# Three norms of a two-layer kernel turned on TensorE by a diagonal of inverse roots, token tile by token tile

## The chip, the cores and the metric

The kernel runs on one core of a Trainium2 chip. Its time is the device time of one execution in microseconds (us), the median of several runs. "Before" is the kernel without the change.

## The reference, cut to what matters

The reference is a transformer layer with attention, a gated delta rule and a product-key expert retrieval, followed by a second layer with two token mixers and a gated feed-forward network. It works on 256 tokens of width 1024. Four times it applies a root-mean-square norm ahead of a large projection:

```python
def rms_norm(x, gain):
    xf = x.astype(jnp.float32)
    y = xf * lax.rsqrt(jnp.mean(xf * xf, axis=-1, keepdims=True) + EPS)
    return (y * gain.astype(jnp.float32)).astype(x.dtype)

h2 = modulate(rms_norm(x, norm2_gain), shift2, scale2)     # h * (1 + scale) + shift, then the expert queries h2 @ w_query
```

The four are: norm 1 (ahead of the first input projection), norm 2 (ahead of the expert queries, with a scale and a shift for every feature), norm 3 (ahead of the second layer's input projection, a gain only) and norm 4 (ahead of the second layer's feed-forward network, a gain only). The change touches norms 2, 3 and 4.

## The kernel before, in words

Tokens are held as two tiles of 128 (tt = 0, 1), with the token on the partition and 1024 features along it. A projection needs its activations with the feature on the partition, so the features are cut into eight K-tiles of 128 (k = 0 to 7), each turned to 128 features by 256 tokens.

**Products in parts.** Every large product is made of three. Both operands are split into a high part, rounded to the type fp32r, and a low part, the rest; high times high, high times low and low times high are summed in PSUM (`three`, L284). The activations' parts are `x_hi` and `x_lo`. The weights arrive in a ring of four chunks, loaded by SyncE (SP). A unit is 128 by 512 weights, and there are eight units for a group of 512 output columns. ScalarE makes a unit's high part (`split_hi`, the copy at L272), VectorE its low part (`split_lo`, the subtraction at L277), into four buffers each. Unit g's buffer is free when TensorE has used unit g - 4. TensorE takes the units in order (`product_group`, L291). In group 0 it waits, ahead of K-tile k, for that K-tile's activation parts (`await_k`) and for the unit's low part (`await_unit`). Each engine's order of work is written out by hand; there is no planner.

**Rows stages.** `rows_stage` (L1265) multiplies row tiles: its output has the tokens on the partition. The last four units are done for token tile 0 first and then for token tile 1, so that VectorE can add tile 0's product to the residual `x` (`add_mix` L1340, `add_wo` L2509, and L1804 and L1805 in the expert stage) while TensorE finishes tile 1. The expert stage has its own code for the same order (L1596 to L1607).

**The norm across a seam.** Each stage is a block of its own. All engines meet where a block ends, before any of them starts the next. At the end of the old block ScalarE loads the table of roots (L456), and then squares each tile of `x` as it becomes ready and takes both square roots in one instruction (L450, L452). In the new block `Norm` does this:

1. VectorE takes both inverses (L472) and scales the rows of tile 0 by its inverse (L474). ScalarE splits unit 0 and then scales the rows of tile 1 (L478).
2. TensorE waits for both (`turn`, L481). It then turns all sixteen 128 by 128 pieces with `pe.transpose` (L362), in four batches of four. A batch is two K-tiles of both token tiles, and a semaphore counts the batches.
3. For each batch, ScalarE writes the high parts of its two K-tiles out of PSUM, with the feature's gain as its scale (L491). Then it splits one weight unit, until four are split. VectorE makes the two low parts (L500; with a shift L505 and L509) and its part of the unit.
4. TensorE starts group 0 as soon as K-tile 0 and unit 0 are there. ScalarE and VectorE go on with unit 4 (`split_groups` L312, and the loops after `norm_his` at L2409 and `norm_los` at L2246).

## Time and profile before

| | |
|---|---|
| time, median of 3 runs (lowest to highest) | 1727.39 us (1727.37 to 1729.22) |
| the profiled execution: its own time, its span | 1728.96 us, 1727.2 us |
| granted TensorE clock over the span | 0.965 of full speed |
| busy, share of the span | TensorE products 92%, weight loads 83%, VectorE 73%, ScalarE 51%, GpSimd 3% |
| three-part products, L287, of 5016 records | 978.6 us busy |
| expert products, L1575, of 3072 records | 386.8 us busy |
| TensorE idle ahead of the turning transposes, L362 | 56.7 us, most of it released by ScalarE's L478 |
| TensorE idle ahead of L287 | 36.5 us, most of it released by VectorE's L277 |

The profile is of one execution. PE is TensorE, PEld its weight loads, DVE VectorE, ACT ScalarE, POOL GpSimd and SP SyncE. "L287" is line 287 of the kernel. A group's line gives the number of records, the busy time, the mean length of one, and then how long the engine sat idle just before them and whose instruction released it. A weight load and a product overlap, and so do successive products, so the mean length of one is more than the distance from one to the next. A plain f32 product leaves two records, a transpose one, and a product of fp32r parts one.

### The profile page before, as it was taken

What the parts mean: (1) busy time and instruction counts of PE and PEld (TensorE: products, weight loads), DVE (VectorE), ACT (ScalarE), POOL (GpSimd) and SP (SyncE); (2) the same over time, 40 slices, a digit from 0 to 9 for tenths busy, and PEclk for the clock granted to TensorE, in tenths of its full rate; (3) what the DMA queues carried; (4) which work ended last, traced back from release to release, by engine and by line L of the source; (5) the groups of instructions that cost most, each with busy time, mean ns of one, the idle gap of its engine ahead of it and who ended that gap; (6) DMA issues with size and microseconds to landing.
All of it is one profiled execution on the core that took longest, in us unless ns stands there. A gap on an engine that the chain in (4) does not pass through costs nothing. (4 is left out here: it accounts for less than half of the span.)

```text
span 1727.2 us, 26513 instructions
## 1 busy us (share of the span) xinstructions
PE 1593.8 (92%) x10380; PEld 1441.4 (83%) x10380; DVE 1257.8 (73%) x2512; ACT 877.8 (51%) x1438; POOL 59.2 (3%) x91
## 2 busy tenths in 40 slices
PE   2997588899999999999999999989999889889989
PEld 2887576799999999998888888888888777789977
DVE  6786877688999899976667766656787566654654
ACT  3436145554554554545555555555555756454443
POOL 0211300000000000000000000020000000000000
PEclk8997789999999999999999999999999899999999
DMA  9744346376766555557777777744444223445542
GB/s 338 268 147 135 104 132 212 99 243 227 235 222 213 181 151 171 149 187 236 240 244 242 243 240 241 250 147 151 149 146 141 73 82 114 146 147 192 176 160 108
DMA packets 112825, 314.45 MB, mean 182 GB/s; under 512 B 8432, under 2 KB 9024, under 8 KB 103232
## 3 DMA queue, kind: packets, MB, share of 16 engines
q1 hardware_dynamic: 101056, 277.03, 48.6%
q10 hardware_dynamic: 10976, 33.63, 5.8%
q0 software_dynamic: 672, 2.12, 0.4%
q8 instruction: 82, 1.34, 0.3%
q14 instruction: 39, 0.32, 0.1%
HBM read 293.86 MB, written 18.89 MB: 181 GB/s over the span
## 5 line engine op out<-in xcount | busy, mean ns | idle before, releaser
L287 PE MATMUL ps<-parts,parts 128*128 128x512 f32 (+1 forms) x5016 | 978.6, 356 | 36.5 <-DVE parts L277 31.0
L287 PEld LDWEIGHTS ps<-parts,parts 128*128 128x128 f32 x5016 | 830.3, 192 | 173.0 <-DVE parts L277 23.7
L272 ACT CAST parts<-lead 128x512 fp32r<-128x512 f32 x940 | 580.5, 621 | 652.7 <-PE ps L287 429.3
L277 DVE TENSOR_TENSOR parts<-lead,parts 128x512 fp32r<-128x512 f32 x940 | 650.2, 698 | 336.9 <-ACT parts L272 333.4
L1575 PE MATMUL ps<-parts,parts 128*128 128x256 f32 x3072 | 386.8, 285 | 4.6 <-DVE parts L277 4.6
L1575 PEld LDWEIGHTS ps<-parts,parts 128*128 128x128 f32 x3072 | 374.1, 192 | 5.6 <-DVE parts L277 5.6
L362 PE MATMUL ps<-lead,mem 128*128 128x128 f32 (+1 forms) x290 | 47.6, 332 | 56.7 <-ACT mem L478 39.7
L362 PEld LDWEIGHTS ps<-lead,mem 128*128 128x128 f32 (+1 forms) x290 | 41.9, 166 | 62.3 <-issue 32.7
L1749 DVE TENSOR_SCALAR mem<-lead,mem 128x128 f32<-128x128 f32 x256 | 71.2, 342 | 0.0
L1561 PE MATMUL ps<-mem 128*128 128x128 f32 x512 | 67.8, 275 | 0.7 <-DVE mem L1749 0.7
L1561 PEld LDWEIGHTS ps<-mem 128*128 128x128 f32 x512 | 62.8, 192 | 1.1 <-issue 1.1
L1746 DVE TENSOR_SCALAR mem<-lead,mem 128x128 f32<-128x128 f32 x256 | 55.6, 281 | 0.0
L1779 DVE TENSOR_TENSOR mem<-mem 128x1024 f32<-128x1024 f32 x32 | 39.0, 1219 | 4.0 <-DMA mem<-act_spill 4.0
L1784 DVE TENSOR_TENSOR parts<-mem,parts 128x1024 fp32r<-128x1024 f32 x32 | 39.0, 1219 | 0.0
L1133 PE MATMUL ps<-mem 64*64 64x64 f32 x512 | 21.0, 251 | 18.1 <-POOL mem L1119 14.4
L1636 ACT COPY mem<-ps 128x512 f32<-128x512 f32 x64 | 37.0, 578 | 0.0
L1632 ACT CAST parts<-mem 128x1024 fp32r<-128x1024 f32 x32 | 33.4, 1045 | 6.6 <-DVE mem L1779 6.6
L1133 PEld LDWEIGHTS ps<-mem 64*64 64x64 f32 x512 | 19.9, 164 | 19.4 <-POOL mem L1119 15.7
L430 DVE SCALAR_TENSOR_TENSOR mem<-mem 128x1024 f32<-128x1024 f32 x27 | 34.5, 1298 | 0.0
L1615 ACT ACTIVATE mem<-ps 128x1024 f32<-128x1024 f32 x32 | 32.6, 1020 | 0.0
L1928 PEld LDWEIGHTS ps<-mem 128*128 128x128 f32 x256 | 29.8, 192 | 0.6
L1928 PE MATMUL ps<-mem 128*128 128x128 f32 x256 | 29.9, 275 | 0.0
(333 smaller groups left out, 969.4 us busy)
## 6 DMA issues: line engine op xcount, KB each, us to landing
lead<-in_peer_expert_down SPq DMA_DIRECT2D x64, 1024.0 KB, 5.6
lead<-in_peer_expert_up SPq DMA_DIRECT2D x64, 1024.0 KB, 5.6
lead<-in_w_in SPq DMA_DIRECT2D x50, 1024.0 KB, 5.1
lead<-in_w_ffn_in SPq DMA_DIRECT2D x22, 1024.0 KB, 5.1
act_spill<-mem ACTq DMA_DIRECT2D x32, 512.0 KB, 5.2
mem<-act_spill ACTq DMA_DIRECT2D x32, 512.0 KB, 3.5
mem<-in_w_ada SPq DMA_DIRECT2D x27, 512.0 KB, 5.2
lead<-in_w_ffn_out SPq DMA_DIRECT2D x11, 1024.0 KB, 4.9
```

The lines of the kernel that those rows point to most:

```text
L272: act.copy(w_hi[g % BUFFERS], st.words(n, u * UNIT, UNIT)).then_inc(hi_ready, 1)
L277: dve.tensor_tensor(w_lo[g % BUFFERS], st.words(n, u * UNIT, UNIT), w_hi[g % BUFFERS].bitcast(F32), ALU.subtract).then_inc(lo_ready, 1)
L287: mm = pe.matmul(o, lhs[a], rhs[b], start=start and i == 0, stop=stop and i == 2, skip_group_check=True, **kw)
L362: last = pe.transpose(o, i, ident[0:i.shape[0], 0:i.shape[0]])
L1133: mm = pe.matmul(ps[rows, bank, u % 4 * HP:(u % 4 + 1) * HP], left[rows, :], right[rows, :], start=True, stop=True)
L1561: mm = pe.matmul(ps[:, 4 + b % 4, j * P:(j + 1) * P], one1[b % 2][:, j, :], one2[b % 2][:, j, :], start=True, stop=True)
L1575: mm = pe.matmul(ps[:, c % 2 * 2 + m // 2, m % 2 * S:(m % 2 + 1) * S], parts[a][:, ms], (x_hi, x_lo)[b][:, k, :], start=k == 0 and i == 0 ...
L1746: one = dve.tensor_scalar(one1[b % 2][:, j, :], iota, pick(0, b * GT + j), None, ALU.is_equal)
L1749: one = dve.tensor_scalar(one2[b % 2][:, j, :], iota, pick(1, b * GT + j), pick(2, b * GT + j), ALU.is_equal, ALU.mult)
L1779: dve.tensor_tensor(got[q % 2], got[q % 2], at(O_R + q * 1024, 1024), ALU.mult).then_inc(s_pr, 1)
L1784: dve.tensor_tensor(a_lo[q], got[q % 2], a_hi[q].bitcast(F32), ALU.subtract).then_inc(s_al, 1)
L1928: mm = pe.matmul(psf[:, 2048 + u * P:2048 + (u + 1) * P], k, q, start=True, stop=True)
```

## The change

A class `TokenNorm` takes the place of `Norm` for norms 2, 3 and 4; norm 1 keeps `Norm`.

- **Roots by tile.** ScalarE squares tile 0 of `x` and takes its root at once, splits weight unit 0 of the next stage, and then does the same for tile 1. All of it is in the old block (`roots`).
- **Diagonals in place of scaled rows.** VectorE takes each tile's inverse and multiplies the 128 by 128 identity by it. It also makes unit 0's low part (`diagonals`, in the old block, behind the two residual sums). The two passes over the rows (L474 and L478) are gone.
- **Turning by products.** In place of sixteen transposes there are sixteen plain f32 products of a 128 by 128 piece of `x` with the tile's diagonal; each turns and scales its piece at once (`turn`). The eight of tile 0 are made at the end of the old block. Four of tile 1 (K-tiles 0 to 3) are made at the start of the new block. The other four are made inside group 0, one behind each of the K-tiles 0 to 3 (`turn_next`).
- **Parts by K-tile.** ScalarE's high part and VectorE's low part are made for one K-tile at a time, each released by a semaphore of that K-tile. Units 1 to 3 are split behind K-tiles 1 to 3, all later units behind K-tile 7 (`his`, `los`). With a shift, VectorE subtracts first and adds the shift in a second instruction.
- In PSUM, K-tiles k and k + 4 share a bank, in banks 4 to 7.

```diff
@@ -308,6 +308,8 @@
                         mm = three(pe, ps[:, c % 2 * 4 + m, 0:S], [w[:, ms] for w in parts],
                                    [a[:, k, :] for a in left], k == 0, k == KT - 1)
                 mm.then_inc(unit_used, 1)
+                if norm and c == 0:
+                    norm.turn_next(pe, k)
         def split_groups(eng, split, at_unit, seg, groups, evacuate, beside=None, done=0):
@@ -387,6 +389,7 @@
         gate1 = at(O_MODS + 2 * D, D)
         c_row = at(O_MODS + 3 * D, D)
         h = at(O_S + D, TT, D)
+        diag = at(O_S, TT, P)
         O_P1 = O_S + 3 * D
         N_P1 = 3 * 512 + 512
         p1 = at(O_P1, TT, N_P1)
@@ -512,6 +515,95 @@
             def await_k(self, pe, k):
                 pe.wait_ge(self.s_lo, k + 1)
+            def turn_next(self, pe, k):
+                pass
+        class TokenNorm:
+            def __init__(self, tag, src, seg, scale, shift=None, less=None):
+                self.src, self.seg, self.scale, self.shift, self.less = src, seg, scale, shift, less
+                (self.s_sq, self.s_std, self.s_inv, self.s_diag, self.s_t, self.s_less, self.s_hi, self.s_lo) = (
+                    lasting_sem(f"{tag}_{n}") for n in (
+                        "squares", "std", "inverse", "diagonals", "transposed", "less_shift", "hi", "lo"))
+            def roots(self, act, s_src):
+                load_roots(act)
+                for tt in range(TT):
+                    act.wait_ge(s_src, tt + 1)
+                    act.activation(h[:, tt, :], self.src[:, tt, :], ACT.Square, accum_out=tiny[:, tt:tt + 1])\
+                        .then_inc(self.s_sq, 1)
+                    act.wait_ge(self.s_sq, tt + 1)
+                    act.activation(tiny[:, 2 + tt:3 + tt], tiny[:, tt:tt + 1], ACT.Sqrt, bias=eps, scale=1.0 / D)\
+                        .then_inc(self.s_std, 1)
+                    if tt == 0:
+                        split_hi(act, self.seg[0], self.seg[1], 0, 0)
+            def diagonals(self, dve):
+                for tt in range(TT):
+                    dve.wait_ge(self.s_std, tt + 1)
+                    dve.reciprocal(tiny[:, 4 + tt:5 + tt], tiny[:, 2 + tt:3 + tt]).then_inc(self.s_inv, 1)
+                    dve.wait_ge(self.s_inv, tt + 1)
+                    dve.tensor_scalar(diag[:, tt, :], ident, tiny[:, 4 + tt:5 + tt], None, ALU.mult)\
+                        .then_inc(self.s_diag, 1)
+                    if tt == 0:
+                        split_lo(dve, self.seg[0], self.seg[1], 0, 0)
+            def column(self, k):
+                return 2048 + k % 4 * 512 + k // 4 * S
+            def bank(self, k):
+                return psf[:, self.column(k):self.column(k) + S]
+            def turn(self, pe, tt, ks):
+                pe.wait_ge(self.s_diag, tt + 1)
+                for k in ks:
+                    col = self.column(k) + tt * P
+                    mm = pe.matmul(psf[:, col:col + P], self.src[:, tt, k * P:(k + 1) * P], diag[:, tt, :],
+                                   start=True, stop=True)
+                    if tt:
+                        mm.then_inc(self.s_t, 1)
+            def his(self, act):
+                for k in range(KT):
+                    act.wait_ge(self.s_t, k + 1)
+                    act.activation(x_hi[:, k, :], self.bank(k), ACT.Identity, scale=self.scale[:, k:k + 1],
+                                   bias=0.0 if self.shift is None else self.shift[:, k:k + 1]).then_inc(self.s_hi, 1)
+                    if 0 < k < AHEAD:
+                        split_hi(act, self.seg[0], self.seg[1] + k, k, 0)
+            def los(self, dve):
+                for k in range(KT):
+                    dve.wait_ge(self.s_hi, k + 1)
+                    rest = x_lo if self.shift is None else self.less
+                    dve.scalar_tensor_tensor(out=rest[:, k, :], in0=self.bank(k), scalar=self.scale[:, k:k + 1],
+                                             in1=x_hi[:, k, :].bitcast(F32), op0=ALU.mult, op1=ALU.subtract)\
+                        .then_inc(self.s_lo if self.shift is None else self.s_less, 1)
+                    if 0 < k < AHEAD:
+                        split_lo(dve, self.seg[0], self.seg[1] + k, k, 0)
+                    if self.shift is not None:
+                        dve.wait_ge(self.s_less, k + 1)
+                        dve.tensor_scalar(x_lo[:, k, :], self.less[:, k, :], self.shift[:, k:k + 1], None, ALU.add)\
+                            .then_inc(self.s_lo, 1)
+            def await_k(self, pe, k):
+                pe.wait_ge(self.s_lo, k + 1)
+            def turn_next(self, pe, k):
+                if k + 4 < KT:
+                    self.turn(pe, 1, (k + 4,))
         class Turn:
@@ -1262,7 +1354,7 @@
-        def rows_stage(tag, seg, chunks, upto, left, dve_part, turn=None, act_after=None, first=None, last=None, beside=None):
+        def rows_stage(tag, seg, chunks, upto, left, dve_part, turn=None, norm=None, s_src=None, first=None, last=None, beside=None):
@@ -1302,6 +1394,8 @@
                     mm.then_inc(s_rows, 1)
                     for i in range(units - 4, units):
                         half(i, 1).then_inc(unit_used, 1)
+                    if norm:
+                        norm.turn(pe, 0, range(KT))
                 @block.scalar
                 def _(act):
@@ -1309,8 +1403,8 @@
                         norm_his(act, turn, seg)
                     for i in range(AHEAD if turn else 0, units):
                         split_hi(act, n0 + i // UPC, g0 + i, i % UPC, 0)
-                    if act_after:
-                        act_after(act)
+                    if norm:
+                        norm.roots(act, s_src)
                 @block.vector
                 def _(dve):
@@ -1329,13 +1423,16 @@
                         else:
                             dve.wait_ge(unit_used, used_value(g0 + units - 1))
                         dve_part(dve, step, tt)
+                    if norm:
+                        norm.diagonals(dve)
         def product_rows(tt, j=0):
             return psf[:, j * 2048 + tt * D:j * 2048 + (tt + 1) * D]
         O_TMP = O_C
-        s_xsum, s_xsq = sem("x1_rows"), sem("x1_squares")
+        s_xsum = sem("x1_rows")
+        norm2 = TokenNorm("norm2", x, n_query, norm_scale, norm_shift, at(O_P1, KT, S))
         def add_mix(dve, step, tt):
@@ -1343,17 +1440,11 @@
             step(dve.tensor_tensor(at(O_TMP + tt * D, D), product_rows(tt), gate1, ALU.mult))
             dve.tensor_tensor(x[:, tt, :], x[:, tt, :], at(O_TMP + tt * D, D), ALU.add).then_inc(s_xsum, 1)
-        def sum_roots(act):
-            load_roots(act)
-            norm_roots(act, h, x, s_xsq, s_xsum)
         def mods_beside_rows(dve, i):
             if i in (5, 7, 9, 11):
                 fill_mods(dve, FILL3 + (i - 5) // 2, FILL3 + (i - 3) // 2)
-        rows_stage("w_out", n_wout, 4, n_query[0] + SLOTS, (x_hi, x_lo), add_mix, Turn("mix1", mix), sum_roots,
+        rows_stage("w_out", n_wout, 4, n_query[0] + SLOTS, (x_hi, x_lo), add_mix, Turn("mix1", mix), norm2, s_xsum,
                    last=lambda sp: load_fills(sp, FILL4 - 3, FILL4), beside=mods_beside_rows)
...
@@ -1404,7 +1494,7 @@
             @block.tensor
             def _(pe):
-                norm2.turn(pe)
+                norm2.turn(pe, 1, range(4))
                 for c in range(4):
                     if c >= 2:
                         pe.wait_ge(s_qv, c - 1)
@@ -1463,7 +1553,7 @@
                     if c and u == 7:
                         scale(c - 1)
-                norm_los(dve, norm2, n_query)
+                norm2.los(dve)
                 split_groups(dve, split_lo, 3, n_query, 4, lambda c: dve.tensor_copy(
                     qrows[:, 0, c * 512:(c + 1) * 512], ps[:, c % 2 * 4, :]).then_inc(s_qv, 1), beside, AHEAD)
                 dve.wait_ge(s_kt, 1)
...
@@ -1605,6 +1696,7 @@
                 mm.then_inc(s_rows, 1)
                 for i in range(2 * P - 4, 2 * P):
                     half(i, 1).then_inc(unit_used, 1)
+                norm3.turn(pe, 0, range(KT))
             @block.scalar
             def _(act):
@@ -1665,8 +1757,7 @@
                         weights_hi(q + 1)
                     if i % 8 == 7 and q + 2 < UG:
                         load_acts(q + 2)
-                load_roots(act)
-                norm_roots(act, h, x, s_xsq, s_xsum)
+                norm3.roots(act, s_xsum)
             @block.vector
             def _(dve):
@@ -1803,6 +1894,7 @@
                         dve.wait_ge(unit_used, used_value(g1 + 2 * P - 1))
                     step(dve.tensor_tensor(x[:, tt, :], psf[:, 2048 + tt * D:2048 + (tt + 1) * D], gate2, ALU.mult))
                     dve.tensor_tensor(x[:, tt, :], x[:, tt, :], x_back[:, tt, :], ALU.add).then_inc(s_xsum, 1)
+                norm3.diagonals(dve)
...
```

Norms 3 and 4 are called in the same way in the second layer's input projection and in the feed-forward stage.

## Rows read from the trace of the kernel before

**Rows 1.** One line of the page's part 5: VectorE's low parts

```profile
L277 DVE TENSOR_TENSOR parts<-lead,parts 128x512 fp32r<-128x512 f32 x940 | 650.2, 698 | 336.9 <-ACT parts L272 333.4
```

**Rows 2.** Timeline where stage `w_out` passes into the query stage: start, length, what [idle before]

```profile
268.22 1.23 DVE L1344 TENSOR_TENSOR mem<-mem 128x1024 f32<-128x1024 f32 x1
...
273.00 3.41 PE L362 MATMUL ps<-lead,mem 128*128 128x128 f32 x16 [6.08 <-ACT mem L478]
...
276.59 3.01 PE L287 MATMUL ps<-parts,parts 128*128 128x512 f32 x12 [0.17 <-DVE parts L509]
...
284.15 8.20 PE L287 MATMUL ps<-parts,parts 128*128 128x512 f32 x35 [0.55 <-DVE parts L277]
```

**Rows 3.** Timeline where the expert stage passes into the second input projection

```profile
1127.61 1.23 DVE L1805 TENSOR_TENSOR mem<-mem 128x1024 f32<-128x1024 f32 x1
...
1130.64 0.17 DVE L472 RECIPROCAL lead<-lead 128x2 f32<-128x2 f32 x1 [1.80 <-PEq L1538]
...
1132.39 3.68 PE L362 MATMUL ps<-lead,mem 128*128 128x128 f32 x16 [6.08 <-ACT mem L478]
...
1133.55 0.84 ACT L491 ACTIVATE parts<-ps,lead 128x256 fp32r<-128x256 f32 x2 [1.21 <-PE ps L362]
...
1134.28 0.62 ACT L272 CAST parts<-lead 128x512 fp32r<-128x512 f32 x1
...
1134.42 0.88 DVE L500 SCALAR_TENSOR_TENSOR parts<-ps,lead,parts 128x256 fp32r<-128x256 f32 x2 [2.22 <-ACT parts L491]
...
1135.72 9.44 PE L287 MATMUL ps<-parts,parts 128*128 128x256 f32 x75
```

**Rows 4.** Timeline where stage `w_o` passes into the feed-forward stage

```profile
1520.26 1.22 DVE L2511 TENSOR_TENSOR mem<-mem,ps 128x1024 f32<-128x1024 f32 x1 [1.50 <-PE ps L287]
...
1525.04 3.48 PE L362 MATMUL ps<-lead,mem 128*128 128x128 f32 x16 [4.81 <-ACT mem L478]
...
1528.17 14.03 PE L287 MATMUL ps<-parts,parts 128*128 128x256 f32 x113
```

**Rows 5.** Short windows in the three seams: the field PEclk is the granted clock

```profile
269.20:269.80 0.60, 0.00 (x0) 0.00 (x0) 0.24 (x1) 0.32 (x1) 0.00 (x0) 0.50 1.03 410
...
276.00:276.50 0.50, 0.41 (x4) 0.17 (x2) 0.50 (x3) 0.50 (x3) 0.00 (x0) 0.99 0.28 74
...
1129.30:1129.60 0.30, 0.00 (x0) 0.00 (x0) 0.00 (x0) 0.30 (x1) 0.00 (x0) 0.57 0.00 0
...
1136.00:1136.40 0.40, 0.40 (x5) 0.40 (x4) 0.40 (x2) 0.40 (x3) 0.33 (x2) 0.79 0.00 0
...
1528.40:1528.80 0.40, 0.40 (x4) 0.40 (x4) 0.40 (x2) 0.40 (x2) 0.00 (x0) 0.62 0.00 0
```

**Rows 6.** Groups of products by line and form, then two lines of VectorE scalars

```profile
L1928 PE MATMUL ps<-mem 128*128 128x128 f32 x256 | 29.9, 275 | 0.0
...
L1166 PE MATMUL ps<-mem 128*128 128x128 f32 x16 | 3.8, 431 | 0.8 <-DVE mem L1232 0.8
...
L1746 DVE TENSOR_SCALAR mem<-lead,mem x256: 274/280/293, 576.9 to 754.7; 128x128 f32<-128x128 f32 x128
...
L2111 DVE TENSOR_SCALAR mem<-mem x8: 404/405/407, 1194.0 to 1196.9; 128x256 f32<-128x256 f32 x8
```

**Rows 7.** Timeline where the projection stage ends: TensorE last before the block's end

```profile
1462.63 4.06 PE L287 MATMUL ps<-parts,parts 128*128 128x512 f32 x17
...
1467.01 1.94 PE L362 MATMUL ps<-lead,mem 128*128 128x128 f32 x16 [0.32 <-PEq L1870]
```

**Rows 8.** Two idle spells of TensorE and the windows with the clock after

```profile
327.36 1.09 PE L362 MATMUL ps<-lead,mem 128*128 128x128 f32 x8 [2.00 <-DVE mem L1450]
...
325.00:330.00 5.00, 1.70 (x14) 1.23 (x13) 4.25 (x9) 2.39 (x6) 0.00 (x0) 1.00 0.00 0
...
1384.72 3.08 PE L362 MATMUL ps<-lead,mem 128*64 128x128 f32 x16 [2.69 <-DVE mem L2219]
...
1385.00:1390.00 5.00, 5.00 (x25) 4.18 (x23) 4.97 (x8) 4.60 (x8) 0.00 (x0) 0.66 0.61 210
```

More of the change, by code:

```diff
@@ L1389, in build @@
                 "qT_dve", "qT_act", "scores", "scores_dve", "scores_act", "steps"))
-        norm2 = Norm("norm2", h, x, norm_scale, norm_shift, at(O_P1, KT, S))
         with nc.Block() as block:
@@ L1495, in beside @@
                         roots(c - 1)
-                norm_his(act, norm2, n_query)
+                norm2.his(act)
                 split_groups(act, split_hi, 4, n_query, 4, lambda c: act.copy(
@@ L1527, in build @@
         n1, g1 = n_up
-        (s_xsum, s_xsq, s_ld, s_rd0, s_rd1, s_pr, s_ah, s_al, s_rows, s_udv) = (sem("up_" + n) for n in (
-            "x_rows", "x_squares", "x_loaded", "acts_loaded0", "acts_loaded1", "weights", "weights_hi", "weights_lo",
+        (s_xsum, s_ld, s_rd0, s_rd1, s_pr, s_ah, s_al, s_rows, s_udv) = (sem("up_" + n) for n in (
+            "x_rows", "x_loaded", "acts_loaded0", "acts_loaded1", "weights", "weights_hi", "weights_lo",
             "rows_done", "steps"))
@@ L1814, in build @@
         O_W = O_P2 + TT * N_P2
-        norm3 = Norm("norm1_2", h, x, gain_cols[:, 2, :])
         HH = 8
@@ L2011, in heads @@
                     mm.then_inc(s_h, 1)
-                norm3.turn(pe)
+                norm3.turn(pe, 1, range(4))
                 for c in range(G_V):
@@ L2244, in gated @@
                         one.then_inc(norm_hg.s_h, 1)
-                norm_los(dve, norm3, n_in2a)
+                norm3.los(dve)
                 for v in range(AHEAD, V_H):
@@ L2407, in weights @@
                     act.activation(zT[j % 2], zT[j % 2], ACT.Exp).then_inc(s_w, 1)
-                norm_his(act, norm3, n_in2a)
+                norm3.his(act)
                 for v in range(AHEAD, V_H):
@@ L2505, in build @@
                    first=mix_hg)
-        s_xsum, s_xsq = sem("x3_rows"), sem("x3_squares")
+        s_xsum = sem("x3_rows")
+        norm4 = TokenNorm("norm2_2", x, n_ffi, gain_cols[:, 3, :])
         def add_wo(dve, step, tt):
             dve.tensor_tensor(x[:, tt, :], x[:, tt, :], product_rows(tt), ALU.add).then_inc(s_xsum, 1)
-        rows_stage("w_o", n_wo, 4, n_ffi[0] + SLOTS, (x_hi, x_lo), add_wo, Turn("mixed_rows", mixed), sum_roots)
-        norm4 = Norm("norm2_2", h, x, gain_cols[:, 3, :])
+        rows_stage("w_o", n_wo, 4, n_ffi[0] + SLOTS, (x_hi, x_lo), add_wo, Turn("mixed_rows", mixed), norm4, s_xsum)
         ff = at(O_F, FT, S)
@@ L2529, in _ @@
             def _(pe):
-                norm4.turn(pe)
+                norm4.turn(pe, 1, range(4))
                 for c in range(2 * FT // 4):
@@ L2554, in high @@
                     act.copy(ff_hi.piece(t), ff[:, t:t + n, :]).then_inc(s_fh, 1)
-                norm_his(act, norm4, n_ffi)
+                norm4.his(act)
                 hi_groups(act, n_ffi, 2 * FT // 4, evacuate, AHEAD)
@@ L2580, in low_part @@
                                       ALU.subtract)
-                norm_los(dve, norm4, n_ffi)
+                norm4.los(dve)
                 lo_groups(dve, n_ffi, 2 * FT // 4, evacuate, AHEAD)
```

1 line of the change is left out of this document (added).

## The prediction

> **What bounds the kernel now.** I read the page's groups first: TensorE works 92% of the span, almost all of it three-part products, so time is lost where it stands still. The waits by releaser then name the spells. Most of its idle time ahead of transposes is put down to ScalarE's L478, which occurs only in the norms. Last I read the timeline of the three seams that the change touches. In the seams of norms 2, 3 and 4 TensorE idles 6.08, 6.08 and 4.81 us [rows 2 to 4]. The stretch from the end of the second residual sum to the first product of group 0 is what the norm costs: 269.45 to 276.59, 1128.84 to 1135.72, and 1521.48 to 1528.17, thus 7.14, 6.88 and 6.69 us [rows 2 to 4]. After that TensorE sets the pace; only in norm 2 does it stall again, and K-tile 4 starts at 284.15 there, 7.56 us after K-tile 0. So the change is priced by one question per norm: when does K-tile 4 start?
>
> **Part by part: up to the first product.** Let E be the end of the second residual sum (VectorE: 269.45, 1128.84, 1521.48). ScalarE has tile 0's root by then, since its square can start when the first sum ends, 2.6 us earlier. VectorE takes the inverse, 0.17 us [rows 3], and the diagonal, a 128x128 scalar pass of 0.28 us [rows 6]. With three handovers of 0.04 us (TensorE starts 0.04 after L478 ends) TensorE starts tile 0 at E + 0.56. ScalarE's second square and root, and VectorE's second diagonal, run beside it and cost nothing as long as tile 0 takes over about 1.5 us; without that cover the second diagonal would come at about E + 2.1.
>
> A 128x128 f32 product takes 29.9/128 = 0.234 us at full clock and 3.8/8 = 0.475 us at the low level, 1.2 GHz, two records each [rows 6]. In a transpose there is less: 1.94/16 = 0.12 us at full clock [rows 7]. The eight thus take 1.87 or 3.80 us. Which? TensorE fell idle at 266.92 and 1126.31; the clock had fallen by 269.20 and at about 1129.35, that is 2.3 and 3.0 us later [rows 5]. Nothing in the change moves these two moments, and tile 0 starts at 270.01 and 1129.40, behind both. The clock came back 3.0, 3.8 and 3.7 us after TensorE had restarted, at 276.0, 1136.17 and 1528.7 [rows 2 to 5]. I take seven products low and one full, 7 x 0.475 + 0.234 = 3.56 us, for norms 2 and 3. In norm 4 there is only one residual pass, so the spell shrinks from 4.81 to 1.22 (the pass) + 0.04 + 0.56 = 1.8 us, less than the 2.00 us at which the clock stayed at 1.00 [rows 8]; the eight take 1.87 us there.
>
> The Trainium skill, "TensorE: Matmul & The Clock Gate", section "Terms", says that transpose mode is four times faster for FP32. The rows give a factor of 2 at equal clock, so the measurement decides. By the page's factor, from a transpose of 0.12, a turning product would be 0.48 at full clock, and the sixteen would add some 4 us per norm.
>
> The block then ends with TensorE last. Where it was last before, the next block's first instruction came 0.32 us after its modelled end [rows 7]. That end lies 0.16 behind the last issue (record of 0.275 less the spacing of 0.117, rows 6). So the new block begins at B = E + 0.56 + 3.56 + 0.48: 274.05 and 1133.44, and for norm 4 with 1.87 at 1524.39.
>
> TensorE makes K-tile 0 of tile 1 in 0.12 + 0.275, ScalarE starts 0.04 later and makes the high part in 0.48 (two take 0.84), VectorE the low part in 0.48 (two take 0.88) [rows 3], and with 0.03 and 0.07 of handovers the first product is at B + 1.5. TensorE's four own products need only 0.94 of it. In norm 2 the shift is a further 0.41 [rows 6] and 0.03. First products: 276.0, 1134.9, 1525.9. They were at 276.59, 1135.72 and 1528.17, so 0.6, 0.8 and 2.3 us are won. The old K-tile 0 began at the low level for its first 0.45 and 0.53 us in norms 3 and 4, which cost half of that; this also goes, 0.2 and 0.3 us.
>
> **Inside group 0.** Four products stand behind K-tiles 0 to 3 in TensorE's own order: 4 x 0.234 = 0.94 us. Nothing hides them, as TensorE has no idle time there. ScalarE has 0.37 + 0.62 per K-tile, VectorE 0.48 + 0.70, with the shift 1.6, against TensorE's 1.5 + 0.23; they keep up.
>
> Then comes a wait that the old order did not have. Unit 4 is split only behind `his` and `los`, whose K-tile 7 needs the last turning product, which TensorE issues behind K-tile 3. Behind this waiting instruction in ScalarE's queue stands `split_hi` of unit 4, and TensorE's K-tile 4 waits for that. Before, the cast of the next unit followed each batch, and unit 4 was ready early. The chain from the end of the issue: 0.16 + 0.04 to ScalarE, 0.37 (half of 1134.28 - 1133.55) to its next instruction, cast 0.62 [rows 3], 0.03, VectorE 0.70 [rows 1], 0.07: 1.98 us idle. In norm 2 VectorE is last: 0.2 + 0.48 + 0.03 + 0.48 + 0.03 + 0.41 + 0.70 + 0.07 = 2.4 us. From K-tile 4 on nothing differs, and the earlier stalls of norm 2 are in the 7.56 us.
>
> **The sum.** Norm 2: 276.0 + 4 x 1.41 (six products, 8.20/35 each, rows 2) + 0.94 + 2.4 = 284.95 against 284.15: +0.8. Norm 3: -0.8 - 0.2 + 0.94 + 1.98 = +1.9. Norm 4: -2.3 - 0.3 + 0.94 + 1.98 = +0.3. Together +3.0 us. The removed passes L474 and L478 are inside these differences. No DMA moves but by the same few tenths; the chunks in question had landed before.
>
> The profiled execution took 1728.96 us, 1.76 beyond its span; it would take 1732.0. The median is 1.6 lower, so I forecast 1727.4 + 3.0 = 1730.4 us.
>
> Bounds of what no row shows. Turning products between fp32r products could hide their weight loads better or worse than in a row of their own: four at 0.12 (a transpose) to 0.475 (the low level) give -0.5 to +1.0 per norm. ScalarE and VectorE read the banks that TensorE writes at that time, which no row has: from 0 to one more product length per K-tile, 0 to 0.9 per norm; I take 0, the four reads of rows 3 having run beside transposes. The one wait per K-tile in place of one per two costs 0 to 4 x 0.04.
>
> **The rivals.**
> 1. The clock does not fall ahead of tile 0. For it: with a restart after 3.1 us the fall may come too late, depending on where in the spell the chip judges it, and 2.00 us left it at 1.00. Against: 2.69 us of idle was followed by a low stretch [rows 8], and both moments in rows 5 lie ahead of the restart. Then norms 2 and 3 are each 1.69 us earlier: 3.0 - 3.4 = -0.4, 1727.0 us, no change.
> 2. The slower side: the new stall at K-tile 4 drops the clock. Idle of 2.00 us left it up, 2.69 us did not [rows 8]; my stalls are 2.0, 2.0 and 2.4 us, so it decides from somewhere between. The window behind the 2.69 us had 0.66, which is 3.4 of 5 us at half rate; TensorE has no slack there and loses 1.7 us each time. Two of three give 3.0 + 3.4: 1733.8 us.
> 3. The change gains as it stands: unit 4 is ready without that wait, because something in the order lets it through. Then 6.4 us of stall go from the sum: -3.4, 1724.0 us. Against it stands the order of instructions itself; ScalarE takes its queue in order in every row.
>
> **How the numbers follow.** Forecast case 0.50, from 1729 to 1732.5; no fall ahead of tile 0 0.20; clock dropped by the stall 0.20; no stall 0.07; the rest 0.03, of either sign. A measurement of this kernel can tell about 0.2%, 3.5 us, from no change. The forecast lies just inside that bound: of its 0.50 I put 0.22 beyond it, and the second rival's 0.20 too, so slower 0.42. Faster is the third rival and half of the rest with a little of the first: 0.10. Same is what is left, 0.48. The range takes in the first rival and its bounds and the second with two or three drops: 1725.5 to 1735.
>
> **What would show it.** Eight f32 product pairs on the new turning line ahead of each block's end, at a PEclk of about 0.5 in norms 2 and 3 and 1.0 in norm 4; the first product of group 0 some 6.5, 6.1 and 4.4 us behind the second residual sum; a turning product behind each of K-tiles 0 to 3; and an idle spell of about 2 us on TensorE ahead of K-tile 4, released by VectorE's L277. The prediction is wrong if that spell is missing or under 1 us, if the turning products take 0.4 us at full clock, or if the clock drops behind the spell.

## The result and the profile after

| | before | changed |
|---|---|---|
| time, median of 22 runs each | 1729.18 us | 1737.97 us |
| lowest to highest | 1724.75 to 1733.54 us | 1729.51 to 1743.32 us |
| ratio to before, 95% interval | | 1.0048 [1.0036, 1.006] |
| the profiled execution: own time, span | 1728.96 us, 1727.2 us | 1742.69 us, 1741.0 us |

The change makes the kernel slower by 0.48%, 8.3 us by the ratio. The forecast was 3.0 us slower, 1730.4 us from a median of three runs. With 22 runs the kernel before has a median of 1729.2 us, so 1.8 us of the miss in the absolute time is that base, and the rest is the change itself.

From the page of the changed kernel, its span and two groups: records and their shapes, busy time, mean ns of one, idle time ahead and its releaser. The first group line answers to the table of the kernel before, the second to [rows 1].

```profile
span 1741.0 us, 26617 instructions
...
L287 PE MATMUL ps<-parts,parts 128*128 128x512 f32 (+1 forms) x5016 | 985.6, 358 | 42.2 <-DVE parts L277 36.3
...
L277 DVE TENSOR_TENSOR parts<-lead,parts 128x512 fp32r<-128x512 f32 x940 | 650.5, 699 | 337.6 <-ACT parts L272 334.0
```

TensorE's idle time ahead of the three-part products grew from 36.5 to 42.2 us. VectorE's low parts cost what they did.

The timeline of the seam of norm 2 (start, length, what, and in brackets the idle time before it and who ended it), which answers to [rows 2]:

```profile
268.90 1.22 DVE L1441 TENSOR_TENSOR mem<-mem 128x1024 f32<-128x1024 f32 x1
...
270.58 3.78 PE L570 MATMUL ps<-mem 128*128 128x128 f32 x16 [2.97 <-DVE mem L554]
...
274.66 2.05 PE L570 MATMUL ps<-mem 128*128 128x128 f32 x8 [0.30 <-PEq L1364]
...
275.46 1.02 ACT L579 ACTIVATE parts<-ps,lead 128x256 fp32r<-128x256 f32 x2 [3.83 <-PE ps L570]
...
276.99 1.65 PE L287 MATMUL ps<-parts,parts 128*128 128x512 f32 x6 [0.28 <-DVE parts L596]
...
283.31 0.38 PE L570 MATMUL ps<-mem 128*128 128x128 f32 x2
...
284.19 2.17 ACT L272 CAST parts<-lead 128x512 fp32r<-128x512 f32 x4
...
285.11 2.49 DVE L277 TENSOR_TENSOR parts<-lead,parts 128x512 fp32r<-128x512 f32 x4
...
285.94 14.37 PE L287 MATMUL ps<-parts,parts 128*128 128x512 f32 x55 [2.26 <-DVE parts L277]
288.16 0.62 ACT L272 CAST parts<-lead 128x512 fp32r<-128x512 f32 x1 [1.81 <-PE ps L287]
...
290.56 0.62 ACT L272 CAST parts<-lead 128x512 fp32r<-128x512 f32 x1 [1.78 <-PE ps L287]
...
291.95 0.62 ACT L272 CAST parts<-lead 128x512 fp32r<-128x512 f32 x1 [0.77 <-PE ps L287]
```

E, the end of the second residual sum, is 268.90 + 1.22 = 270.12. Tile 0's products start 0.46 behind it, take 3.78 us (low clock), and the first product of group 0 comes at E + 6.87. Behind the last turning product TensorE stands idle for 2.26 us until VectorE has unit 4's low part. Then the reader is to look at ScalarE's casts at 288.16, 290.56 and 291.95. Each is released by TensorE's use of a unit. Two of them are 2.40 us apart and the next two 1.39, so in the first of these two intervals TensorE ran at about half its rate. The clock fell at about 286.9, 0.9 us after TensorE had restarted.

The seam of norm 3, to be read beside [rows 3]: TensorE's pieces and two casts.

```profile
1134.34 3.78 PE L570 MATMUL ps<-mem 128*128 128x128 f32 x16 [2.97 <-DVE mem L554]
...
1138.42 1.97 PE L570 MATMUL ps<-mem 128*128 128x128 f32 x8 [0.30 <-PEq L1629]
...
1140.27 1.70 PE L287 MATMUL ps<-parts,parts 128*128 128x256 f32 x12
...
1149.06 16.12 PE L287 MATMUL ps<-parts,parts 128*128 128x256 f32 x120 [1.89 <-DVE parts L277]
...
1153.46 0.62 ACT L272 CAST parts<-lead 128x512 fp32r<-128x512 f32 x1 [1.89 <-PE ps L287]
...
1155.14 0.62 ACT L272 CAST parts<-lead 128x512 fp32r<-128x512 f32 x1 [1.05 <-PE ps L287]
```

And that of norm 4, beside [rows 4]:

```profile
1534.74 2.05 PE L570 MATMUL ps<-mem 128*128 128x128 f32 x16 [1.71 <-DVE mem L554]
...
1537.09 1.13 PE L570 MATMUL ps<-mem 128*128 128x128 f32 x8 [0.30 <-PEq L1364]
...
1538.63 1.70 PE L287 MATMUL ps<-parts,parts 128*128 128x256 f32 x12 [0.42 <-DVE parts L589]
...
1547.42 12.82 PE L287 MATMUL ps<-parts,parts 128*128 128x256 f32 x105 [1.89 <-DVE parts L277]
```

In norms 3 and 4 the wait ahead of K-tile 4 is 1.89 us. Short windows behind the three waits show the clock (the field behind the four engines' busy times and counts, as in [rows 5]):

```profile
286.60:290.10 3.50, 3.50 (x11) 2.67 (x10) 1.70 (x3) 0.62 (x1) 0.00 (x0) 0.54 0.31 75
...
1151.00:1154.30 3.30, 3.30 (x19) 3.30 (x18) 0.88 (x2) 1.19 (x2) 0.00 (x0) 0.57 0.72 215
...
1547.40:1551.00 3.60, 3.58 (x30) 3.60 (x31) 2.38 (x4) 1.77 (x4) 0.00 (x0) 1.00 0.20 30
```

It was 0.54 and 0.57 of full speed behind the waits of norms 2 and 3, and 1.00 behind that of norm 4.

From the profiles I took the length of each seam: from E to the start of VectorE's low part of unit 12, where both kernels are in the same steady state again.

```
us                   norm 2  norm 3  norm 4   sum     against before
before               22.52   21.03   20.94   64.49
changed              25.27   24.83   21.38   71.48    +7.0
units_early          21.18   21.34   19.25   61.77    -2.7
before_held          25.42   22.71   23.66   71.79    +7.3
before_held_long     26.00   24.78   25.68   76.46   +12.0
tile0_late           22.38   22.45   22.85   67.68    +3.2
after_filled         23.65   23.45   21.38   68.48    +4.0
before_shift         23.45   20.72   20.86   65.03    +0.5
units_early_warm     19.13   19.18   19.26   57.57    -6.9
before_warm          23.93   21.48   21.46   66.87    +2.4
before_warm_short    22.32   19.90   19.89   62.11    -2.4
held_filled          23.78   22.68   22.92   69.38    +4.9
norm4_alone          22.51   21.24   22.88   66.63    +2.1
```

This is one profiled execution of each, so the table shows mechanisms and the timed runs show sizes. What a low stretch behind the wait is worth can be read from pairs with the same order of work, one with and one without it: 25.27 - 23.65, 24.83 - 23.45 and 22.88 - 21.38, thus 1.4 to 1.6 us. Of the 13.7 us between the profiled executions of before and changed, 7.0 lie in the three seams. Most of the rest lies in later stages that the change doesn't touch: from unit 12 of the queries to the expert stage 59.39 against 57.26, in the rest of the second input projection 231.84 against 230.40, and from there to norm 4's second residual sum 101.61 against 99.10. There too it is the clock: its mean in these three stretches is 0.91 against 0.97, 0.95 against 0.96 and 0.98 against 1.00, because low stretches stand at other idle spells.

Every timed execution has its mean granted clock as well. I call 2 x (1 - clock) x span its low time, the time at the lower level. Averaged over the executions it is 118.7 us for the changed kernel (22 of them). For the kernel before, in the three later sets of runs, it is 115.2, 113.3 and 112.9 us (17, 35 and 26 executions). Within one kernel its standard deviation is 5 to 15 us, so an average of twelve is good to some 2 to 4 us. A TensorE at half its rate loses half of that time where it has work to do.

### The profile page after: what moved, and what is told of

Read it like the earlier page. It is cut to its first block and busy times, and to the rows that moved or that the text cites. A ratio compares the mean times of both kernels' runs of the same rounds, so it can differ in the third digit from the quotient of the medians.

```text
span 1741.0 us, 26617 instructions
## 1 busy us (share of the span) xinstructions
PE 1610.4 (92%) x10428; PEld 1455.7 (84%) x10428; DVE 1257.9 (72%) x2518; ACT 875.5 (50%) x1438; POOL 57.3 (3%) x91
## 5 line engine op out<-in xcount | busy, mean ns | idle before, releaser
L287 PE MATMUL ps<-parts,parts 128*128 128x512 f32 (+1 forms) x5016 | 985.6, 358 | 42.2 <-DVE parts L277 36.3
L277 DVE TENSOR_TENSOR parts<-lead,parts 128x512 fp32r<-128x512 f32 x940 | 650.5, 699 | 337.6 <-ACT parts L272 334.0
L364 PE MATMUL ps<-lead,mem 128*128 128x128 f32 (+2 forms) x242 | 37.6, 319 | 39.4 <-ACT mem L481 22.6
L364 PEld LDWEIGHTS ps<-lead,mem 128*128 128x128 f32 (+2 forms) x242 | 32.9, 157 | 43.7 <-issue 32.8
```

The costliest lines, as they stand in the source:

```text
L277: dve.tensor_tensor(w_lo[g % BUFFERS], st.words(n, u * UNIT, UNIT), w_hi[g % BUFFERS].bitcast(F32), ALU.subtract).then_inc(lo_ready, 1)
L287: mm = pe.matmul(o, lhs[a], rhs[b], start=start and i == 0, stop=stop and i == 2, skip_group_check=True, **kw)
L364: last = pe.transpose(o, i, ident[0:i.shape[0], 0:i.shape[0]])
```

## The experiments

**units_early.** Units 4 to 7 are split where units 1 to 3 are; the loops behind start at unit 8.

```diff
-                    if 0 < k < AHEAD:
-                        split_hi(act, self.seg[0], self.seg[1] + k, k, 0)
+                    if k:
+                        split_hi(act, self.seg[0] + k // UPC, self.seg[1] + k, k % UPC, 0)
...
-                for v in range(AHEAD, V_H):
+                for v in range(KT, V_H):
```

> The changed kernel with one thing different: in norms 2 to 4, weight units 4 to 7 are split behind K-tiles 4 to 7, as units 1 to 3 are behind theirs, and not all behind K-tile 7. Theory 1 (the wait at K-tile 4 and the low clock behind it are the loss): the idle spells of 2.26, 1.89 and 1.89 us ahead of K-tile 4 go, 6.0 us, and with them the low stretches that follow some of them, 1.7 us each. Against the changed kernel's 1738.0 that gives 8 to 9 us less, 1729 to 1730; counted from the kernel before and the seams alone it would be 1729.2 + 3.0 - 6.4 = 1725.8. Rival (the loss is in the turning products, or in low stretches far from the seams that have nothing to do with the wait): at most the 6.0 us of idle time, 1732 or more, and low stretches in group 0 as before.

Measured: 1730.79 us (12 runs), ratio to before 1.0006 [0.9989, 1.0023]. TensorE's timeline at K-tile 4 of norm 2 has no gap left; the last turning product is issued 0.14 us ahead of K-tile 4's first:

```profile
282.90 0.38 PE L570 MATMUL ps<-mem 128*128 128x128 f32 x2
283.04 17.29 PE L287 MATMUL ps<-parts,parts 128*128 128x512 f32 x75
```

Its seams are 9.7 us shorter than the changed kernel's. By the ratios to before it is 0.42% faster, 7.3 us. That lies between the 8 to 9 us of theory 1 and the at most 6.0 of the rival, so the time alone doesn't decide; that no low stretch is left in group 0 speaks for theory 1. The wait at K-tile 4 and what follows it are the loss; taken away, nothing is left that can be told from before. The count from the seams alone, 1725.8, was too good: the seams are 2.7 us shorter than before, and the total is not. In its profile the three later stretches named above took 59.94, 232.03 and 101.72 us, 6.9 us more than before, at the same lower clocks as in the changed kernel.

**before_held and before_held_long.** The kernel before, computing the same, with a wait at the same place in each of norms 2, 3 and 4 and nothing else of the change (256 or 1024 columns in the copy; norm 2's is shown):

```diff
                 norm_his(act, norm2, n_query)
+                act.wait_ge(unit_used, used_value(n_query[1] + 3))
+                act.copy(at(O_S, 256), at(O_CONST, 256))
```

> The kernel before with one wait added in each of norms 2, 3 and 4: ScalarE splits unit 4 only when TensorE has used unit 3, behind a copy of 128x256 that nobody reads (0.4 us). It computes the same. That holds TensorE ahead of K-tile 4 for about 0.2 + 0.4 + 0.62 + 0.03 + 0.70 + 0.07 = 2.0 us, as the changed kernel does, with nothing else of the change. Theory 1 (a wait of this length also brings the low clock in part of the cases): 3 x 2.0, less norm 2's own earlier waits, and up to 3 x 1.7: 1729.2 + 8.5 = 1737.7, with low stretches seen behind one or two of the three waits. Rival (the wait costs its own length only): 1735.2 and PEclk 1.00 behind all three.

> The same with a copy of 128x1024 (1.0 us), so that TensorE is held about 2.6 us ahead of K-tile 4 in each of norms 2 to 4. Theory 1: the low clock follows all three waits, 3 x (2.6 + 1.7) = 12.9: 1742, which is 4 to 5 above the shorter hold although the waits are only 1.9 us longer together. Rival: 1.9 us above the shorter hold.

Measured: 1738.69 us (6 runs), 1.0067 [1.0055, 1.0079], and 1741.32 us (6 runs), 1.0082 [1.0067, 1.0097]. The timeline of before_held at norm 2 has the added copy and a wait of 1.83 us:

```profile
282.44 0.40 ACT L1499 COPY mem<-lead 128x256 f32<-128x256 f32 x1 [4.17 <-PE ps L287]
...
284.23 8.01 PE L287 MATMUL ps<-parts,parts 128*128 128x512 f32 x27 [1.83 <-DVE parts L277]
```

Windows right behind the three waits of before_held (PEclk as before), and then of before_held_long, whose waits are 2.47 us:

```profile
284.90:288.40 3.50, 3.50 (x10) 2.69 (x9) 1.68 (x3) 0.64 (x2) 0.00 (x0) 0.51 0.45 113
1146.30:1149.80 3.50, 3.49 (x29) 3.50 (x30) 2.36 (x4) 1.66 (x4) 0.00 (x0) 1.00 0.17 30
1541.20:1544.70 3.50, 3.49 (x29) 3.50 (x30) 2.36 (x4) 1.66 (x4) 0.00 (x0) 1.00 0.15 30
```

```profile
281.50:285.00 3.50, 3.50 (x9) 2.79 (x10) 1.61 (x3) 1.20 (x3) 0.00 (x0) 0.53 0.23 34
1145.00:1148.50 3.50, 3.50 (x19) 3.50 (x19) 0.92 (x3) 1.24 (x2) 0.00 (x0) 0.52 0.64 205
1544.20:1547.70 3.50, 2.81 (x13) 2.84 (x14) 2.35 (x4) 1.39 (x3) 0.00 (x0) 0.52 0.00 0
```

In these profiles the clock was low behind one of three waits of 1.83 us and behind all three of 2.47. before_held loses 11.6 us where its waits add 1.28 + 1.83 + 1.83 = 4.9 us (in norm 2 there was a stall of 0.55 before). That is more than theory 1's 8.5 and far above the rival's 6.0. Its low time is 127.4 us against 115.2 for before in the same set of runs, 12.2 more, and half of that is 6.1. A wait of this kind costs more than its length, and alone it costs at least as much as the whole change. The longer wait didn't separate theory 1 from its rival: it is 2.6 us above the shorter one, where 4 to 5 were expected and the rival said 1.9, the intervals overlap, and its low time is no longer (125.9 us).

**tile0_late.** As units_early, with tile 0's products moved into the new block.

```diff
-                    if norm:
-                        norm.turn(pe, 0, range(KT))
...
+                norm2.turn(pe, 0, range(KT))
                 norm2.turn(pe, 1, range(4))
```

> As units_early, but token tile 0's eight turning products stand at the start of the new block, ahead of the four of tile 1, and not at the end of the old one. Theory 1 (the early tile gains what the seams were worked out to gain): the new block then begins when the second diagonal is there, 2.35 us behind the second residual sum, and the first product of group 0 comes at 2.35 + 3.6 + 1.5 = 7.4 us in norms 2 and 3 (6.9 in the changed kernel, both at the low clock) and at 5.7 to 7.4 in norm 4 (4.3): 2.4 to 4 us above units_early. Rival (the early tile gains nothing, as the same eight products stand in TensorE's way wherever they are): within 1 us of units_early.

Measured: 1734.9 us (6 runs), 1.0037 [1.0023, 1.0051], 0.31% or 5.4 us above units_early. In norm 2 all twelve products start 4.87 us after TensorE fell idle, and the first product of group 0 is 1.2 us later than in units_early (276.56):

```profile
272.01 4.95 PE L570 MATMUL ps<-mem 128*128 128x128 f32 x24 [4.87 <-PEq L1364]
277.76 1.66 PE L287 MATMUL ps<-parts,parts 128*128 128x512 f32 x6 [0.80 <-DVE parts L596]
```

So the early tile does gain something: the seams say 5.9 us and the totals 5.4, where 2.4 to 4 were expected, though the two intervals just touch. In norm 4 the longer idle spell let the clock fall; that seam alone grew by 3.6 us.

**after_filled.** The changed kernel, with products that nobody reads in the wait:

```diff
                 if k + 4 < KT:
                     self.turn(pe, 1, (k + 4,))
+                if k == 3:
+                    for _ in range(14):
+                        pe.matmul(psf[:, 1792:2048], x_hi[:, 0, 0:P], x_hi[:, 0, :], start=False, stop=True, skip_group_check=True)
```

> The changed kernel with TensorE kept busy in the wait ahead of K-tile 4: behind the last turning product, fourteen 128x256 products of fp32r parts (0.12 us each, 1.7 us) into an unused corner of PSUM that nobody reads. The wait itself stays, 1.9 to 2.3 us until unit 4's low part is there. Theory 1 (part of the loss is the low clock that follows the idle spell): no low stretch behind the three waits, so up to 1.7 us less for each that had one; the seams of norms 2 and 3 (25.3 and 24.8 us from the second residual sum to the low part of unit 12) fall to about 23.5 and 23.1, the total by 2 to 5 us, to 1733 to 1736. Rival (the wait costs its own length and nothing else): 1738 as the changed kernel.

Measured: 1732.78 us (12 runs), 1.0014 [0.9999, 1.0029]. K-tile 4 of norm 3 waits as long as before, but TensorE is idle for 0.22 us of it only:

```profile
1143.57 1.92 PE L609 MATMUL ps<-parts 128*128 128x256 f32 x14
1145.71 19.55 PE L287 MATMUL ps<-parts,parts 128*128 128x256 f32 x161 [0.22 <-DVE parts L277]
```

Against the changed kernel, by the ratios to before, that is 0.34%, 5.9 us less (the two intervals together leave some 3 us on either side), with the same waits in the order of work. What is left above before is 2.4 us, and the sum of the prediction, which has no low stretch behind the new wait, was 3.0. This is the run that splits the loss: about 6 us are the clock behind the wait, about 3 the rest. The granted clocks of the single executions agree. Low time was 118.7 us on average over the 22 executions of the changed kernel and 106.8 us over the 12 of this one, 11.9 us less, and half of that is 6.0 us. The Trainium skill, "TensorE: Matmul & The Clock Gate", section "Terms", puts the penalty at about the throttled time multiplied by one less the clock ratio. Here the two agree, 6.0 by the clocks and 5.9 by the times.

The 3 us that are left are not free of the clock. In the kernel before, the clock was low for 3.4 us in norm 4's transposes, and in the changed kernel it is not (the table's 21.38 us has no low stretch); the prediction's sum counts that as a gain. All in all this run has 6.5 us less low time than before in the same set of runs (106.8 against 113.3). By half of it, an estimate, the order of work alone costs nearer to 6 us, and a better clock gives 3 of them back.

**held_filled.** before_held with the same fill, behind K-tile 3.

```diff
                 mm.then_inc(unit_used, 1)
+                if norm and c == 0 and k == 3 and norm is not norm1:
+                    for _ in range(14):
+                        pe.matmul(psf[:, 1792:2048], x_hi[:, 0, 0:P], x_hi[:, 0, :], start=False, stop=True, skip_group_check=True)
```

> before_held (the kernel before, with K-tile 4 held some 2.0 us in norms 2 to 4) with the fourteen 128x256 products that nobody reads behind K-tile 3 in TensorE's order, so that the wait is of the same length and TensorE is busy in it. Theory 1: what before_held loses beyond the waits themselves is the low clock, so this one loses 5.3 (the growth of idle time ahead of K-tile 4 in the three seams): 1729.5 + 5.3 = 1734.8 or a ratio of 1.003, against 1.0067 for before_held. Rival (the held unit costs more than its wait in some other way, such as units split late behind it): 1.006 to 1.007 as before_held.

Measured: 1734.08 us (9 runs), 1.0031 [1.0016, 1.0047], as theory 1 had it. Norm 2 of it:

```profile
283.35 1.83 PE L313 MATMUL ps<-parts 128*128 128x256 f32 x14
285.34 14.98 PE L287 MATMUL ps<-parts,parts 128*128 128x512 f32 x65 [0.17 <-DVE parts L277]
```

The wait is the same and costs 5.4 us now in place of 11.6. The same fill gives back 6 us in a kernel that has nothing of the change but the wait. That the 5.4 are the waits' own 4.9 is less sure than it looks: low time is 106.6 us, against 127.4 in before_held, but also against 112.9 for before in the same set of runs. So here too some clock was gained that before didn't have, and something else, which no run names, took it back.

**before_shift.** A copy of 1.0 us behind norm 2's roots.

```diff
             norm_roots(act, h, x, s_xsq, s_xsum)
+            if s_xsum is x1_sum:
+                act.copy(at(O_S + D, 1024), at(O_CONST, 1024))
```

> The kernel before with one copy of 128x1024 (1.0 us) more on ScalarE behind norm 2's roots, so that everything from norm 2 on comes 1.0 us later, and nothing else. Theory 1a (what the changed kernel loses outside the three seams comes from low stretches that move when the stages behind are moved): the total changes by 1.0 plus or minus 1.7 or 3.4, and the low stretches of the later stages stand elsewhere than in the kernel before. Rival (the difference outside the seams is chance between executions): 1.0 us more on average, 1728.8 to 1730, with the same spread.

Measured: 1729.62 us (12 runs, 1724.86 to 1736.26), 1.0003 [0.9986, 1.0019]; seam of norm 2 0.93 us longer. Inconclusive: the interval holds no effect and the 1.0 us, and no later stage of its profile differs by more than about 0.4 us from before. That merely moving the later stages costs time is not shown.

**units_early_warm.** units_early, with TensorE kept busy ahead of tile 0's products.

```diff
                     for i in range(units - 4, units):
                         half(i, 1).then_inc(unit_used, 1)
+                    if norm:
+                        for _ in range(12 if seg == n_wout else 7):
+                            pe.matmul(psf[:, 2048:2560], left[0][:, 0, 0:P], atr(O_X_HI, KT * S)[:, 0:512], start=True, stop=True)
```

> units_early with TensorE kept busy in the spell ahead of tile 0's turning products: 128x512 products that nobody reads, twelve in norms 2 and 3 (2.6 us) and seven in norm 4 (1.5 us), behind the stage's last product. Theory 1 (the low clock makes tile 0's eight products 3.8 in place of 1.9 us in norms 2 and 3): first product of group 0 about 1.7 us earlier in both, seams of 19.5, 19.6 and 19.3 us, 1730.8 - 3.5 = 1727.3 and less if later low stretches go too. Rival (the fill stands in TensorE's queue ahead of the turning products and eats what the clock gives): within 1 us of units_early.

Measured: 1723.73 us (12 runs), 0.9965 [0.9948, 0.9983]. This beats both kernels, before by 0.35% and the changed one by 0.83%. Its norm 2:

```profile
263.49 2.88 PE L1399 MATMUL ps<-parts 128*128 128x512 f32 x12
...
266.62 2.05 PE L570 MATMUL ps<-mem 128*128 128x128 f32 x16 [0.25 <-DVE mem L554]
...
268.97 1.13 PE L570 MATMUL ps<-mem 128*128 128x128 f32 x8 [0.30 <-PEq L1364]
...
270.99 1.66 PE L287 MATMUL ps<-parts,parts 128*128 128x512 f32 x6 [0.89 <-DVE parts L596]
```

Tile 0 takes 2.05 in place of 3.78 us, and all three seams are within 0.2 us of each other: none has a low stretch. Tile 0 starts 0.45 us behind the second residual sum, as it did without the fill, so the fill stood in nobody's way. The gain over units_early, 0.41% or 7.1 us, is twice the 3.5 expected; the seams give 4.2 of it.

**before_warm and before_warm_short.** The kernel before with such a fill ahead of its transposes, 26 and 20 products, then 19 and 13.

```diff
+                    if act_after:
+                        for _ in range(19 if seg == n_wout else 13):
+                            pe.matmul(psf[:, 2048:2560], left[0][:, 0, 0:P], atr(O_X_HI, KT * S)[:, 0:512], start=True, stop=True)
```

> The kernel before with the same fill ahead of the turning transposes: 26 products of 128x512 in norms 2 and 3 (5.6 us of the 6.1), 20 in norm 4 (4.3 us of 4.8). The sixteen transposes then run at full clock, 1.9 in place of 3.4 us, and the first product comes 0.8 to 1.6 us earlier. Theory 1: 1729.2 - 3 x 1.2 = 1725.6, and less if low stretches in later stages go. Rival: the clock is of no matter here because VectorE's low parts set the first product: within 1 us of before.

> before_warm with its mistake mended: there TensorE's fill was still running when all other engines had reached the block's end, which held the block back by some 1.6 us in each seam. Nineteen products of 128x512 in norms 2 and 3 (4.1 us) and thirteen in norm 4 (2.8 us) end ahead of that point and leave TensorE idle for 2.0 us ahead of the transposes. Theory 1: transposes mostly at full clock, seams of norms 2 to 4 each 0.5 to 1.5 us shorter than before (22.5, 21.0, 20.9), total 1729.5 - 3 = 1726.5. Rival (VectorE's low parts and the per-batch order set the first product, not the clock): within 1 us of before.

Measured: 1734.38 us (12 runs), 1.0019 [1.0003, 1.0035], and 1728.77 us (12 runs), 0.9997 [0.9983, 1.0012]. TensorE in norm 2, first of before_warm, then of before_warm_short:

```profile
267.02 6.05 PE L1307 MATMUL ps<-parts 128*128 128x512 f32 x26
275.12 2.82 PE L362 MATMUL ps<-lead,mem 128*128 128x128 f32 x16 [2.05 <-ACT mem L478]
```

```profile
266.68 4.47 PE L1307 MATMUL ps<-parts 128*128 128x512 f32 x19
273.19 1.97 PE L362 MATMUL ps<-lead,mem 128*128 128x128 f32 x16 [2.05 <-ACT mem L478]
276.32 3.02 PE L287 MATMUL ps<-parts,parts 128*128 128x512 f32 x12 [1.16 <-DVE parts L509]
```

The long fill ends at 273.07, after all other engines had come to the block's end. It holds the block back: the transposes start at E + 5.42 where they were at E + 3.56, 1.9 us late, so before_warm only measures a fill that was sized wrongly. The short one still ends a little late (E + 3.83, 0.3 us); its transposes take 1.97 us at full clock, and yet the first product is at 276.32, E + 6.96 where it was E + 7.14: TensorE then idles 1.16 us for VectorE's low part. The seams of norms 3 and 4 did become 1.1 us shorter each, but of that nothing can be told from before in the total. Theory 1's 1726.5 was missed, and the rival was right for norm 2 and for the total.

**norm4_alone.** The changed kernel with norms 2 and 3 in the old form (a class that gives `Norm` the new calls).

```diff
-        norm3 = TokenNorm("norm1_2", x, n_in2a, gain_cols[:, 2, :])
+        norm3 = OldNorm("norm1_2", x, n_in2a, gain_cols[:, 2, :])
```

> The changed kernel with norms 2 and 3 in their old form; only norm 4 has the diagonal, the turning products and the wait at K-tile 4. Theory 1: its seam is 0.4 us longer, with 1.7 more where a low stretch follows the wait; nothing with idle spells but the feed-forward's end comes behind it, so 1729.9 to 1731.5. Rival (each of the three norms has a third of the loss): +2.8, 1732.3.

Measured: 1730.82 us (12 runs), 1.0013 [1.0001, 1.0025], 2.2 us more. Its interval reaches from 0.2 to 4.3 us and holds theory 1 and the rival. In its profile the wait of norm 4 was followed by a low stretch, as it was not in the changed kernel's own profile, and the seam is 22.88 us where that one's is 21.38:

```profile
1528.05 0.39 PE L570 MATMUL ps<-mem 128*128 128x128 f32 x2
1530.32 19.85 PE L287 MATMUL ps<-parts,parts 128*128 128x256 f32 x151 [1.89 <-DVE parts L277]
```

## Why the prediction was wrong

**Up to the first product: right but for 0.4 us.** Forecast were 6.5, 6.1 and 4.4 us behind the second residual sum; they came at 6.87, 6.37 and 4.34. The clock was low for tile 0 in norms 2 and 3 and full in norm 4, as I had taken it: 3.78, 3.78 and 2.05 us for the eight. It came back later than taken, though: in norm 2 at about 276.6, 6.0 us after TensorE's restart and not 3 to 4. So all eight products were slow and most of tile 1's four too (2.05 us where norm 4 has 1.13), which is where the 0.3 to 0.4 us in norms 2 and 3 come from. The transition between blocks with TensorE last took its 0.30.

**Inside group 0: right.** A turning product inside group 0 took 0.22 us (the K-tiles of norm 3 are 1.66 apart in place of 1.44), so the four cost 0.9. The wait at K-tile 4 was there, released by VectorE's L277, and had 2.26, 1.89 and 1.89 us where 2.4, 1.98 and 1.98 were worked out.

**The sum: right for what it held.** after_filled keeps the whole change and takes only the low clock behind the wait away; it measures +2.4 us against the +3.0 of the sum, and before_held with its wait filled measures +5.4 where the waits add 4.9. Part of that closeness is luck: the interval of after_filled reaches from -0.2 to +5.0 us, and both filled kernels have less low time than the kernel before, which the sum held only for norm 4.

**What failed** is the term that the sum put at nothing: the clock behind the new stall at K-tile 4. "From K-tile 4 on nothing differs", says the part on group 0. The second rival, that the stall drops the clock, got only 0.20 and no place in the forecast, because one spell of 2.00 us had left the clock at 1.00 and my stalls were shorter or only a little longer [rows 8]. In its place the runs showed some 6 us: filling the stall gives back 5.9 us in the changed kernel and 6 in before_held. The profile of the changed kernel has a low stretch behind spells of 2.26 and 1.89 us, before_held behind one of 1.83. One row of a spell that left the clock up is no bound: the same 1.89 us was followed by a low stretch in norm 3 and not in norm 4, and in norm 4 of another execution it was. The place of that rival was right, and its price nearly: 1.7 us for a drop, where pairs of seams give 1.4 to 1.6. With all three drops it gives 3.0 + 3 x 1.7 = 8.1 us, and the ratio says 8.3. That this fits so well is luck, as the one profile of the changed kernel shows two drops behind the waits, not three.

The rival also ended too low as a time and the range with it: the text says that the range takes in three drops, and it doesn't quite. Three drops from the median of three runs give 1735.5, above the range's end of 1735; from the median of 22 runs they give 1737.3.

**Still open** is how the 6 us of clock divide. One execution's profile had two drops behind the waits, 3.4 us, and more low stretches in later stages. The fill gives back 5.9 us where three drops of 1.7 would be 5.1, which the spread of the executions allows. Whether the later stages suffer from the change, or had them by chance in that execution, before_shift did not settle. The longer form of the three later stretches stands in the profiles of the changed kernel and of units_early, the form of before in those of after_filled, before_shift and norm4_alone.

## What to carry to other kernels

Ask of every new wait on TensorE not only how long it is but what the clock does behind it. Here waits of 1.8 to 2.3 us cost on average about twice their length, because behind some of them TensorE ran at 1.2 GHz for 3.4 us, and filling the waits with products that nobody reads gave some 6 us of 8 to 12 back. If parts of an operand are made K-tile by K-tile, the split of the weights has to be interleaved through to the last K-tile; when one engine's in-order queue holds the last K-tile's work ahead of the next unit's, the pipeline drains once per seam. And a rearrangement can be worth having once its one bad wait is out: the same turning by products, without the wait and with a busy TensorE ahead of it, is 0.35% faster than the kernel before.

## What the runs showed of the hardware that was not expected

- The clock fell behind idle spells of 1.83, 1.89 and 2.26 us, and stayed at 1.00 behind others of 1.83, 1.89 and 2.00 us, so the length of the spell does not decide it alone. Behind three spells of 2.47 us it was low each time, in one execution. Behind six spells of 2.05 us, in before_warm and before_warm_short, it fell once: after norm 2's in before_warm, 0.9 us after the restart.
- Products that nobody reads kept the clock up, and they were free in time where they ended before TensorE was needed, the end of a block included: 0.25 us of idle time ahead of tile 0 in units_early_warm against 2.97 in the changed kernel's norm 2, and a tile of 2.05 in place of 3.78 us.
- A 128x128 f32 product between products of fp32r parts cost 0.22 us, in a row of its own 0.23. VectorE's scalar pass of 128x256 from SBUF into fp32r took 0.35 us where 0.41 was taken.
